# A two-block transformer kernel: weight slots refilled across block borders, and the causal term of the token attention moved to VectorE

## The reference

```
def causal_attention(q, k, v):             # 12 heads, d = 96, 1024 tokens
    scale = 1.0 / math.sqrt(d)
    sc = einsum(q_blk, k) * scale
    mask = k_pos[None, :] <= q_pos[:, None]
    sc = jnp.where(mask, sc, -jnp.inf)
    p = softmax(sc)
    return einsum(p, v)
# 32 of the 96 rows of q and k are turned by the rotary embedding:
#   [t1 * cos - t2 * sin, t1 * sin + t2 * cos]
```

## Time and profile before

| what | value |
|---|---|
| median of three runs | 3357.79 us |
| profiled execution: its time, its span | 3356.56 us, 3354.4 us |
| PE busy | 3075.8 us, 92% of the span |
| DVE, ACT, POOL busy | 1304.9, 976.9, 808.8 us |
| token attention, 2440 to 2812 us: PE, DVE, ACT, POOL busy | 348.9, 229.4, 139.5, 67.0 of 372 us, granted clock 0.99 |
| one head of it, between the starts of its S and of the next | 31.75 us |
| mask products L3182 in all (96 products, two records each) | 37.3 us; one is 0.22 us of PE's stream |
| DVE in a head: L3270, L3271, L3272, L3273 | 1.22, 1.23, 1.22, 2.73 us |
| DVE's maxima L3241 over 128, 256, ..., 1024 columns | 0.29, 0.42, 0.56, 0.68, 0.82, 0.96, 1.09, 1.23 us |
| ACT, 512, 384, 256, 128 columns of exponential; copies of 1024 columns | 0.60, 0.49, 0.38, 0.28 us; 1.0 us |

### The profile page before, as it was taken

One profiled execution on the slowest core, in us unless ns is written; L12 is line 12 of the kernel. 1 busy time (PEld: TensorE's weight loads), 2 busy tenths in 40 slices (PEclk: granted clock), 3 DMA queues, 4 the chain that ended last, 5 costly groups with the idle time before them and its releaser, 6 DMA issues. The chain is left out here.

```text
span 3354.4 us, 33625 instructions
## 1 busy us (share of the span) xinstructions
PE 3075.8 (92%) x14024; PEld 2304.5 (69%) x14024; DVE 1304.9 (39%) x1342; ACT 976.9 (29%) x1264; POOL 808.8 (24%) x380
## 2 busy tenths in 40 slices
PE   8899999999989888899999999898789998889886
PEld 3677777877766476688888787676456666667555
DVE  5153111333425443300000245230656664528555
ACT  3232222212134123311111344332133431337312
POOL 1222111214332122322222345322021211223100
PEclk9999999999989899899999999998799999999897
DMA  9311111252132352111111233312100001121201
GB/s 359 132 51 63 51 51 57 107 176 76 57 114 99 108 182 69 51 50 44 46 48 50 70 109 124 114 53 85 57 13 20 20 13 69 63 69 38 91 13 50
DMA packets 76485, 261.01 MB, mean 78 GB/s; under 512 B 8048, under 2 KB 12384, under 8 KB 75328
## 3 DMA queue, kind: packets, MB, share of 16 engines
q1 hardware_dynamic: 76352, 259.13, 22.0%
HBM read 207.10 MB, written 51.99 MB: 77 GB/s over the span
## 5 line engine op out<-in xcount | busy, mean ns | idle before, releaser
L277 POOL TENSOR_TENSOR w_lo_sb<-raw_w_sb,w_hi_sb 128x1024 fp32r<-128x1024 f32 x231 | 578.5, 2505 | 2052.1 <-ACT w_hi_sb L268 2052.0
L268 ACT ACTIVATE w_hi_sb<-raw_w_sb 128x1024 fp32r<-128x1024 f32 x231 | 243.1, 1052 | 437.2 <-PE ps L285 401.6
L285 PE MATMUL ps<-merged_parts_hi_sb,w_hi_sb 128*128 128x512 f32 x832 | 336.1, 404 | 22.6 <-PEq L500 12.1
L285 PE MATMUL ps<-merged_parts_lo_sb,w_hi_sb 128*128 128x512 f32 x832 | 332.1, 399 | 0.0
L285 PE MATMUL ps<-h_hi_sb,w_hi_sb 128*128 128x512 f32 x720 | 297.3, 413 | 18.2 <-PEq L872 11.2
L285 PE MATMUL ps<-h_lo_sb,w_hi_sb 128*128 128x512 f32 x720 | 289.1, 401 | 0.0
L285 PE MATMUL ps<-merged_parts_hi_sb,w_lo_sb 128*128 128x512 f32 x832 | 273.0, 396 | 0.0
L285 PE MATMUL ps<-h_hi_sb,w_lo_sb 128*128 128x512 f32 x720 | 246.1, 401 | 0.0
L285 PE MATMUL ps<-z_lo,w_hi_sb 128*128 128x512 f32 x512 | 206.3, 403 | 0.0
L285 PEld LDWEIGHTS ps<-merged_parts_hi_sb,w_hi_sb 128*128 128x128 f32 x832 | 158.2, 190 | 68.1 <-issue 18.6
L2732 DVE TENSOR_TENSOR ffn_hidden_sb<-ffn_hidden_sb,ps 128x1024 f32 x20 | 24.4, 1221 | 431.4 <-PE ps L285 431.4
(11 more groups left out here) (571 smaller groups left out, 5569.8 us busy)
## 6 DMA issues: line engine op xcount, KB each, us to landing
raw_w_sb<-in_w SPq DMA_DIRECT2D x231, 512.0 KB, 3.2
ada_w_sb<-in_ada SPq DMA_DIRECT2D x48, 512.0 KB, 7.5
inbox_sb<-gates_out SPq DMA_DIRECT2D x24, 512.0 KB, 4.1
gates_out<-outbox_sb SPq DMA_DIRECT2D x16, 512.0 KB, 2.6
inbox_sb<-sums_out SPq DMA_DIRECT2D x16, 512.0 KB, 4.7
spilled_sum<-x_sb SPq DMA_DIRECT2D x32, 256.0 KB, 2.0
x_sb<-spilled_sum SPq DMA_DIRECT2D x2, 4096.0 KB, 13.8
x_sb<-in_x SPq DMA_DIRECT2D x4, 1024.0 KB, 10.9
```

The source lines that it names most:

```text
L268: nc.scalar.activation(w_hi[:, n % RING].rearrange("p t m -> p (t m)"), raw_w[:, n % RAW], ACT.Copy).then_inc(w_rounded.sem, 1)
L277: nc.gpsimd.tensor_tensor(w_lo[:, n % RING].rearrange("p t m -> p (t m)"), raw_w[:, n % RAW], flat_hi, ALU.subtract).then_inc(w_split.sem, 1)
L285: mm = nc.tensor.matmul(o, wt, xs, start=start and part == 0 and xs is x_hi, stop=stop and part == 1)
```

## The change

**Refills.** `dense` takes `keep=1`: the refill of its last slot is left out of the part and put on a list, and `refill()` issues it as a part of the next block, whichever kind that is: ACT's L268 at planned time 0.2, POOL's L277 at 1.4, SP's fetch at 4.0 after the block's start (in `linear` and in the memory attention ahead of their own work). Eleven parts get it, those of the table.

**Token attention.** The second matmul for the causal term goes; DVE adds `mask_kq` to the scores in PSUM (`causal_term`), and ACT's exponential of a diagonal block waits for DVE. The second half's key blocks come in the order 4, 5, 6, 7, 0, 1, 2, 3, so that the diagonal blocks are steps 0 to 7. The product with the values is two steps behind, not one. The three rotary instructions of head u+1 stand between the causal terms of head u; the cast is ACT's now (`round_turned`, after the exponential of step 4). The next head's maxima are at steps 5 (two of them) to 11. `gating.high` (a rounding of the gated output on ACT, every other head) is after step 8's exponential at the new place.

```diff
+        def refill():
+            slots = list(left)
+            left.clear()
+            def on_sp(sp):
+                for n in slots:
+                    yield 4.0
+                    if n + RAW < n_slots:
+                        sp.wait_ge(w_split.sem, n + 1)
+                        sp.dma_start(raw_w[:, n % RAW], a["w"][n + RAW]).then_inc(w_full[n % RAW].sem, 16)
+            def on_act(act, link):
+                for n in slots:
+                    yield 0.2
+                    round_slot(act, None, n, 0)
+            def on_pool(pool, link):
+                for n in slots:
+                    yield 1.4
+                    rest_of_slot(pool, None, n, 0)
+            return Part(on_sp, None, on_act, None, on_pool)
+
         def side_by_side(*parts):
+            parts = (refill(),) + parts
+            for p in parts:
+                left.extend(p.left)
...
                 if e == "act":
-                    todo += [(event, 1, sl) for sl, event in slot_at.items()]
+                    todo += [(event, 1, sl) for sl, event in slot_at.items() if sl < slots - keep]
...
-                for sl in range(slots):
+                for sl in range(slots - keep):
                     yield time_of[slot_at[sl]] + 1.4
                     rest_of_slot(pool, None, s0 + sl + RING, slots)
...
+            part.left = [s0 + sl + RING for sl in range(slots - keep, slots)]
...
-                steps = [(u, t, s) for u in range(U) for t in range(2) for s in range(4 * t + 4)]
+                blocks = ((0, 1, 2, 3), (4, 5, 6, 7, 0, 1, 2, 3))
+                steps = [(u, t, s) for u in range(U) for t in range(2) for s in blocks[t]]
...
+                            behind = 2 if causal else 1
...
-                                        if diag:
-                                            mm = nc.tensor.matmul(ps[:, 4 + n % 2, 0:P], ident, C("mask_kq"),
-                                                                  start=False, stop=True)
...
-                                        if n > mine[0]:
-                                            weigh(n - 1)
+                                        if n - mine[0] >= behind:
+                                            weigh(n - behind)
                                         if causal and u + 1 < U:
-                                            if 2 <= n - mine[0] < 2 + CH:
-                                                maxima(u + 1, n - mine[0] - 2)
+                                            for b in {5: (0, 1), 6: (2,), 7: (3,), 8: (4,), 9: (5,), 10: (6,), 11: (7,)
+                                                      }.get(n - mine[0], ()):
+                                                maxima(u + 1, b)
+                                    if causal:
+                                        weigh(mine[-2])
...
+                        def round_turned(u):
+                            act.wait_ge(dve_free.sem, b_e["dve"] + after["dve"][at[("Q", u, 0)]])
+                            nc.scalar.activation(rounded(u)[0][64:96], q_of(u)[64:96], ACT.Copy).then_inc(rounded_s.sem, 1)
...
+                            def causal_term(n):
+                                dve.wait_ge(pe_s.sem, b_s + n + 1)
+                                nc.vector.tensor_tensor(ps[:, 4 + n % 2, 0:P], ps[:, 4 + n % 2, 0:P], C("mask_kq"), ALU.add
+                                                        ).then_inc(causal_s.sem, 1)
...
-                                    nc.vector.tensor_copy(rounded(u)[0][64:96], q_).then_inc(dve_free.sem, 1)
...
+                                        for j in range(CH):
+                                            causal_term(step_at[(u, 0, 0)] + j)
+                                            if 1 <= j <= 3 and 1 < u + 1 < U:
+                                                turn_queries(u + 1, j - 1)
+                                            if u + 1 < U:
+                                                for b in {5: (0, 1), 6: (2,), 7: (3,)}.get(j, ()):
+                                                    take_maxima(i, u + 1, b)
                                     normalise(i, u, 0)
-                                        for b in range(2, CH):
+                                        for b in range(4, CH):
                                             take_maxima(i, u + 1, b)
```

More of the change, by code:

```diff
@@ L129, in __init__ @@
         self.sp, self.pe, self.act, self.dve, self.pool = sp, pe, act, dve, pool
+        self.left = ()
 def ordered(*programs):
@@ L323, in linear @@
             order = {e: [u for u in range(U) if plan[u] == e] for e in ("act", "dve")}
+            refilled = refill()
             with nc.Block() as block:
@@ L327, in _ @@
                 def _(sp):
+                    together([refilled.sp(sp)])
                     if iters == 1:
@@ L568, in claim, with dense @@
             return [(free[f].sem, v) for f, v in before.items()]
-        def dense(at, nm, kt, rhs, plan, emit, banks, pace=1.0, store=None, jobs=None, needs=None, due=None):
+        def dense(at, nm, kt, rhs, plan, emit, banks, pace=1.0, store=None, jobs=None, needs=None, due=None,
+                  keep=0):
             s0, base = stream["slot"], pe_done.n
@@ L669, in on_pool @@
             def on_pool(pool, link):
-                for sl in range(slots):
+                for sl in range(slots - keep):
                     yield time_of[slot_at[sl]] + 1.4
                     rest_of_slot(pool, None, s0 + sl + RING, slots)
-            fetch = prefetch(s0, slots, [time_of[slot_at[sl]] for sl in range(slots)])
+            fetch = prefetch(s0, slots - keep, [time_of[slot_at[sl]] for sl in range(slots)])
             def stores(sp):
@@ L1516, in rows @@
                 rows_written.n += 32
-            side_by_side(heads_in, gate_to_memory(heads_in.end, 0, outbox, PAIRS, 1.4), scores(), Part(rows))
+            side_by_side(heads_in, gate_to_memory(heads_in.end, 0, outbox, PAIRS, 1.4, 1), scores(), Part(rows))
             finish(kv_written)
@@ L1691, in outputs @@
                 return Part(None, on_pe, on_act, on_dve)
-            side_by_side(values, gate_to_memory(values.end, 1, outbox, PAIRS, 1.3), outputs())
+            side_by_side(values, gate_to_memory(values.end, 1, outbox, PAIRS, 1.3, 1), outputs())
             over([(rest_s, 1), (grown_s, 1), (last_s, 1), (fall_s, 1), (turned_s, 1), (keys_t, 4), (keys_s, 4),
@@ L2931, in build @@
             latents = dense(ends[1], 4, 8, from_h, ["act"] * 4, emit, PAIRS, jobs=EARLY_HALVES, needs=there,
-                            due=[ends[1], H_AT[1] + 13.0])
+                            due=[ends[1], H_AT[1] + 13.0], keep=1)
             def kept(sp):
@@ L3001, in attention @@
             if causal:
-                steps = [(u, t, s) for u in range(U) for t in range(2) for s in range(4 * t + 4)]
-                last = lambda t: 4 * t + 3
+                blocks = ((0, 1, 2, 3), (4, 5, 6, 7, 0, 1, 2, 3))
+                steps = [(u, t, s) for u in range(U) for t in range(2) for s in blocks[t]]
+                begins = lambda t: 4 * t
+                last = lambda t: 3
             else:
                 steps = [(u, t, s) for u in range(U) for t in range(2) for s in range(keys_n // P)]
+                begins = lambda t: 0
                 last = lambda t: keys_n // P - 1
             step_at = {st: n for n, st in enumerate(steps)}
+            on_diagonal = [causal and s >= 4 * t for _, t, s in steps]
+            diagonals = [sum(on_diagonal[:n + 1]) for n in range(len(steps))]
             span = lambda t, s: (max(HALF * t, P * s) if causal else HALF * t, HALF * (t + 1))
@@ L3035, in looped, with _ @@
                             body(i)
+                refilled = refill()
+                assert not (causal and left)
                 with nc.Block() as block:
+                    if not causal:
+                        @block.sync
+                        def _(sp):
+                            together([refilled.sp(sp)])
+                        @block.gpsimd
+                        def _(pool):
+                            together([refilled.pool(pool, None)])
                     if causal:
@@ L3108, in weigh @@
                                 pe.wait_ge(act_p.sem, val(i, len(steps), b_p + n + 1))
-                                if s == 0 and (g >= 2 or i is not None):
+                                if s == begins(t) and (g >= 2 or i is not None):
                                     pe.wait_ge(dve_o.sem, val(i, 2 * U, b_do + g - 1))
                                 nc.tensor.matmul(ps[:, 6 + t, lo - HALF * t:HALF], v_of(u, s), pr[:, n % 4, 0:hi - lo],
-                                                 start=(s == 0), stop=(s == last(t))).then_inc(pe_o.sem, 1)
+                                                 start=(s == begins(t)), stop=(s == last(t))).then_inc(pe_o.sem, 1)
                             def turn_values(u):
@@ L3290, in body @@
                                 if kind == "S":
```

(10 more changed lines are left out.)

71 lines of the change are left out of this document (45 added, 26 removed).

## The result

The changed kernel takes 3337.16 us (median of 4 runs, 3334.85 to 3338.14) against 3357.09 for the kernel before in the same series: a ratio of 0.9934, 95% interval 0.9919 to 0.9949, so 20 us faster. The forecast was 3320 us, with a range of 3303 to 3340. The direction holds and the time is inside the range, but two terms of the sum are wrong, and they cancel in part: the borders gave more than I said, and the attention, which I had as a gain of 9 us between bounds of -21 and +8, is a loss of 19. So that the time lies inside the range is in part luck.

A forecast was written before the change was run, and what follows sets the result against it. PE, busy 92% of the span, was taken as the bound; 3356.6 us less 23.8 (borders' idle), 4.2 (clock) and 9 (attention) gave 3319.6, said as 3320 us, range 3303 to 3340.

The forecast's parts named there:

- Borders, idle time: PE's idle time at the eleven borders falls by 23.8 us in sum, bounds 16 to 28.
- Borders, clock: Clock behind five borders: kept at 1410 and 2991, 4.2 us gained; lost at the three others; bounds 0 and 10.9.
- Causal term: DVE's addition in PSUM in the token attention takes 0.28 us, between 0.28 and 0.69.
- Steady head: A middle attention head of 31.75 us gets 0.8 us shorter, of 0.5 to 1.3; the attention 9 us.
- the walk: Three queues timed through stage S of an attention head: 23.6 us new, 24.2 old, -0.5 a head.
- The step that failed: In an attention head POOL is done at 6.2 us, DVE's piece with two SBUF operands starts at 6.1: nothing lost.
- my own sign: The forecast counts as wrong if an attention head takes over 31.75 us.
- rival (4): DVE falls behind in the attention: causal term 0.69 or piece locked out, 1.5 us a head; 3337 us, chance 0.08.
- Rival (3): The borders give half, as something no row separates takes the freed place: 12 us less, 3332 us; chance 0.10.
- rival (5): DVE's causal term takes 1.2 us: attention +3.6 us a head, +40 in all, 3369 us; chance 0.04.
- Rival (1): The clock holds behind all five borders: a further 6.7 us go, 3313 us; chance 0.17.
- rival (2): The attention becomes PE's stream with no new waits: -21 us instead of -9, 3308 us; chance 0.11.

The follow-up runs named there:

- run 1: Changed kernel with the old token attention put back, refills still moved at eleven borders: 3325.6 us, 0.9902 of the kernel before.
- the ten traces above: Ten traces of kernels with these refills moved, the changed kernel's among them; the clock behind the border at 2179 was 0.72 in six, 1.00 in four.
- run 5: As run 3, but the causal term is PE's second matmul again: 3322.8 us, 0.9899 of the kernel before.
- run 3: Changed kernel, with POOL's `z_lo` subtraction waiting until ACT has rounded the turned queries: 3321.2 us, 0.9898 of the kernel before.
- run 4: Changed kernel, with POOL's subtraction of the weight slot done twice in the short heads: 3346.8 us, 0.9971 of the kernel before.
- run 7: As run 1, with POOL's slot subtraction waiting until DVE has rounded the turned queries: 3319.0 us, 0.9891 of the kernel before.
- run 6: As run 3, with ACT's cast after the exponential of step 3 and the maxima at steps 5 to 10: 3309.1 us, 0.9856 of the kernel before.
- run 8: As run 3, with `keep=1` taken from `og`, the part before the border at 998: 3323.4 us, 0.9899 of the kernel before.

## Why the prediction was right, and where it was wrong

**Borders, idle time: right.** At seven of the eleven borders the forecast is within 0.15 us of the measured one: at six of them it was the difference of two columns, at 2336 my choice between 1.1 and 3.4. I gave 0 at 1176 and 1230, and 1.5 and 1.0 came. Both are the lock, seen from its good side: with the refill gone, DVE's last addition ahead of the border no longer stands beside POOL's subtraction. DVE before and after at 1230, and POOL before (its L277 ran from 1223.92 to 1226.27):

```profile
1225.28 2.06 DVE L1268 TENSOR_TENSOR inbox_sb<-inbox_sb 128x1024 f32<-128x1024 f32 x1
```

```profile
1214.22 1.23 DVE L1304 TENSOR_TENSOR inbox_sb<-inbox_sb 128x1024 f32<-128x1024 f32 x1
```

2.06 became 1.23, and at 1176 the same instruction went from 1.91 to 0.69, which with the stores behind it is what those borders gave. I had seen this effect at 3160 (L3923) and priced it there alone. At 998 I charged ACT's 1.05 in full, and it cost nothing, because ACT is not what PE waits for there. PE's first matmul needs DVE's `y_parts_lo`, and DVE comes to it only after three instructions that start when `ml_f` has landed. Before:

```profile
993.34 1.06 ACT L2180 ACTIVATE y_parts_hi_sb<-y_sb 128x1024 fp32r<-128x1024 f32 x1
993.68 0.74 DVE L2426 TENSOR_SCALAR ml_G<-ml_G,vec_sb 4x1024 f32<-4x1024 f32 x1 [2.04 <-DMA ml_f<-rows_out]
...
996.38 1.20 DVE L2184 TENSOR_TENSOR y_parts_lo_sb<-y_sb,y_parts_hi_sb 128x1024 fp32r<-128x1024 f32 x1
```

and after:

```profile
978.84 0.90 DVE L2462 TENSOR_SCALAR ml_G<-ml_G,vec_sb 4x1024 f32<-4x1024 f32 x1 [1.59 <-DMA ml_f<-rows_out]
...
980.10 1.06 ACT L2216 ACTIVATE y_parts_hi_sb<-y_sb 128x1024 fp32r<-128x1024 f32 x1
...
981.69 1.20 DVE L2220 TENSOR_TENSOR y_parts_lo_sb<-y_sb,y_parts_hi_sb 128x1024 fp32r<-128x1024 f32 x1
```

ACT's rounding is done 2.0 us ahead of DVE's subtraction before and 0.5 ahead of it after: the slot fits into that gap. Sum 28.7 of 23.8 forecast.

**Borders, clock: right in kind, small in size.** The two that I took as kept were kept. The others were not all lost: 5 matmuls more at the first border, 3 at the second, 1 at 2179, at 0.19 us each some 2 us, beside the 4.2. That makes 35 us; outside the attention the changed kernel's trace is 37 us shorter than the one before, and run 1, the borders alone, is 31 us faster, against 28 forecast. At 2179 it was a toss-up, as the ten traces above show. (My 1.9 for that border does not follow from its count: 10 matmuls in 3.91 us lose 1.6, and the bound of 10.9 is 10.6.)

**Causal term: right.** 0.298 against 0.28, and 0.5 us a head gained by it (run 5). That it costs 2 us in the first head I had not seen.

**Steady head: the walk gave -0.5, I took -0.8, the short heads show -0.15.** The walk had PE's new waits at 1.2, 0.9 and 0.55; the trace has 1.43, 0.68 and 0.41. The places were right. What I added to the walk (the old order's short last steps) was a wish: I should have stayed with -0.5.

**The step that failed** is this sentence: "By the rows nothing is lost: POOL is done 6.2 us after the start of S". It is true of POOL's slot, and POOL's queue has a second instruction behind it in every other head, `z_lo`, which the timeline of the kernel before shows in the very head that I read:

```profile
2611.88 2.79 POOL L3724 TENSOR_TENSOR z_lo<-z_sb,z_hi 128x1024 fp32r<-128x1024 f32 x1
```

I weighed the port's lock against one instruction and put it in a rival at 0.08, with 1.5 us a head. It comes in five heads at 3 us each, since PE's wait then reaches 2.8 us and the clock falls: +15 in the attention. Beside it, the first head is 2.8 longer (the clock stays at half for 10 us behind the wait of 10.7 us, for the 10.5 of before, where the old order had it back after 4), the last two together 1.6 longer, three short heads are 0.15 shorter each, the one at 32.8 is 1.0 longer (its clock fell 4 us after its start, behind no wait over 0.15 us), and the first head starts 1.5 sooner. Together 18.8.

The lock is not all of the miss. Without it (run 3) the attention is still 3.2 us longer than before, where I had 9 less: the first head is 3.1 longer instead of 0.6 shorter, the last two together 0.8 longer instead of 1.3 shorter, and the nine between gain 0.5 in all, 2.2 without the fall of the clock in one of them, instead of 7. By my own sign, a head over 31.75, I was wrong on the attention.

The Trainium skill, "SBUF — State Buffer", "SBUF: two separate sides", has the shared pair as "an exclusive lock, not a bandwidth split", held for the whole instruction. Runs 3, 4 and 7 agree: 1.22 or 2.62 for the same addition, 0.68 or 2.73 for the same cast, by nothing but what POOL does. By that rule, applied to all of POOL's queue, the attention would have come out at -5.5 + 15 = +9.5 (an estimate, from the walk's -0.5 in eleven heads and five long heads at the 3 us that the runs show): a loss, as it was, of half its size.

**The rivals.** The mechanism was half of rival (4), with 3 us in five heads where it had 1.5 in each; that its 3337 is the measured time is chance, since the borders gave more. Rival (3), that the borders give half, is refuted (run 1); rival (5), a dear causal term, too. Rival (1), that the clock holds behind all five borders, and rival (2), an attention with no new waits, did not come.

## What to carry to other kernels

Before an instruction with two SBUF operands on VectorE is moved, or an SBUF to SBUF cast, lay POOL's whole queue beside the new place, not only the instruction that you know: one overlap cost 1.4 us on top of an addition of 1.22. A wait of one queue for the other can be worth as much as the rewrite around it: it gave 16 us in run 3, and 4.5 us of the attention in run 7, beside which the whole rewrite at its best (run 6) gives 4.7 more. Compare a rewrite with the old code after the same remedy. A refill that nobody needs for three slots has no business in front of a barrier; there PE's idle time falls by the difference between the last two instructions ahead of it (within 0.15 us at six borders). And a wait has a second price: each of the five waits of 2.8 us in the changed kernel's heads was followed by a fall of the clock worth 1.7 us or more, while of the twenty waits of 1.4 in runs 3 and 8 one was.

## What the runs showed of the hardware that I had not expected

Which engine has to wait seems to be decided by hundredths of a microsecond. One addition (DVE's L2251, inputs and output in SBUF) took 2.75 us where POOL's subtraction started 0.22 before it (changed kernel, 1017.50), 2.90 where it started 0.01 before (run 6, 1014.66), and 0.69 where both starts read 1017.80 (run 4); there POOL's took 2.93 instead of 2.35. The clock behind the wait of 10.5 to 10.7 us came back after 4 us in the kernel before and after 10 in the changed one, with PE busy all the time in both: 26 matmuls in the second 4 us against 17. It goes with the causal term, and not with the order of the steps, which run 5 has too: with the term on PE (before, runs 1, 5 and 7) the first head took 32.9 to 34.1 us, with it on DVE (all eight other traces) 34.5 to 36.1. Why stays open. And traces of identical instructions differ by up to 5 us in a stretch of 200 (138 to 344), so that a sum over stretches says more than the whole time.
